# Gated linear attention: ScalarE copies the two widest levels' scores of heads 0 to 3

## The reference

```python
def gla_chunk_scan(q, k, v, log_f):
    """S_t = diag(f_t) S_{t-1} + k_t^T v_t ; o_t = q_t S_t."""
    G = jnp.cumsum(to_c(log_f), axis=3)
    ...
        o_inter = jnp.einsum('bhtk,bhkv->bhtv', qt * jnp.exp(Gt), state)
        decay = jnp.where(causal, jnp.exp(jnp.where(causal, diff, 0.0)), 0.0)
        attn = jnp.einsum('bhtk,bhsk,bhtsk->bhts', qt, kt, decay)
        o_intra = jnp.einsum('bhts,bhsv->bhtv', attn, vt)
```

## Time and profile before

| | |
|---|---|
| time, median of 3 runs | 1917.98 us (1917.0 to 1919.4) |
| the profiled execution's own time | 1920.67 us |
| its span in the trace | 1919.0 us |
| TensorE busy (matmul) | 1874.8 us, 98% |
| VectorE busy | 1177.9 us, 61% |
| ScalarE busy | 1041.1 us, 54% |
| GpSimd busy | 375.9 us, 20% |

### The profile page before, as it was taken

The page is one execution under the profiler, slowest core; times in us unless marked ns, Lnnn a source line. Parts: engine busy times, 40 slices in busy tenths (PEclk is TensorE's granted clock), DMA queues, the critical chain, the costliest instruction groups (busy, mean ns, idle before and its releaser), DMA issues.

```text
span 1919.0 us, 27344 instructions
## 1 busy us (share of the span) xinstructions
PE 1874.8 (98%) x10047; PEld 1629.7 (85%) x10047; DVE 1177.9 (61%) x2462; ACT 1041.1 (54%) x1810; POOL 375.9 (20%) x453
## 2 busy tenths in 40 slices
PE   7999999999999999999999999999999999999998
PEld 7987877788788777689999999999888887778887
DVE  3335389754799999875454554445343645957972
ACT  5654543444588887764545554555443565445440
POOL 1601233101001100132122332133020102402310
PEclk9999999999999999999999999999999999999999
DMA  4411222118699999932333233333343512122131
GB/s 155 142 56 45 67 66 67 48 63 286 215 369 360 359 372 355 333 116 61 91 84 94 80 84 93 84 90 104 98 142 112 177 55 77 56 66 77 56 110 44
DMA packets 187312, 259.44 MB, mean 135 GB/s; under 512 B 14605, under 2 KB 101594, under 8 KB 187178
## 3 DMA queue, kind: packets, MB, share of 16 engines
q1 hardware_dynamic: 178048, 225.56, 36.5%
q0 software_dynamic: 8720, 31.59, 4.4%
q10 hardware_dynamic: 410, 0.52, 0.1%
HBM read 239.24 MB, written 14.16 MB: 132 GB/s over the span
## 4 chain that ended last, share of the span: by engine, by line
PE 71%; DVE 18%; DMA 5%; ACT 3%; issue 2%; SPq 1%; POOL 0%; ACTq 0%; DVEq 0%; POOLq 0%
PE pb L2644 53%; DVE wlo L1732 7%; PE pb L2671 5%; DMA wraw<-w_down 4%; PE pb L2730 2%; PE pb L2743 2%; PE pb L3171 1%; ACT whi L1065 1%; PE pb L3279 1%; PE pb L3037 1%; SPq L796 1%; DVE arena L1993 1%; DVE AT_lo L2100 1%; PE pb L2911 1%; DVE small L1992 1%
## 5 line engine op out<-in xcount | busy, mean ns | idle before, releaser
L2644 PE MATMUL pb<-whi,AT_hi 128*128 128x512 f32 (+4 forms) x1864 | 724.8, 389 | 1.9 <-DVE arena L1928 0.8
L1732 DVE TENSOR_TENSOR wlo<-wraw,whi 128x1024 fp32r<-128x1024 f32 (+4 forms) x430 | 493.9, 1163 | 300.0 <-ACT whi L1065 297.5
L2644 PE MATMUL pb<-whi,AT_lo 128*128 128x512 f32 (+4 forms) x1864 | 677.2, 363 | 0.0
L2644 PE MATMUL pb<-wlo,AT_hi 128*128 128x512 f32 (+4 forms) x1864 | 676.1, 363 | 0.0
L1065 ACT ACTIVATE whi<-wraw 128x1024 fp32r<-128x1024 f32 (+4 forms) x446 | 440.6, 995 | 354.8 <-PE pb L2644 306.7
L2644 PEld LDWEIGHTS pb<-whi,AT_hi 128*128 128x128 f32 x1864 | 352.6, 189 | 44.3 <-issue 9.0
L2644 PEld LDWEIGHTS pb<-wlo,AT_hi 128*128 128x128 f32 x1864 | 352.9, 189 | 39.4 <-issue 6.8
L2644 PEld LDWEIGHTS pb<-whi,AT_lo 128*128 128x128 f32 x1864 | 351.6, 189 | 39.8
L2671 PE MATMUL pb<-arena 128*128 128x128 f32 (+1 forms) x956 | 144.6, 276 | 6.3 <-ACT arena L1159 2.8
L2671 PEld LDWEIGHTS pb<-arena 128*128 128x128 f32 (+1 forms) x956 | 118.2, 142 | 34.8 <-issue 7.9
L3037 PE MATMUL pb<-whi,AT_hi 128*128 128x512 f32 x256 | 104.9, 410 | 2.0 <-DVE wlo L1732 1.2
(11 more groups left out here) (363 smaller groups left out, 2624.8 us busy)
## 6 DMA issues: line engine op xcount, KB each, us to landing
wraw<-w_in_a SPq DMA_DIRECT2D x288, 128.0 KB
wraw<-w_gate SPq DMA_DIRECT2D x128, 256.0 KB
wraw<-w_up SPq DMA_DIRECT2D x128, 256.0 KB
wraw<-w_down SPq DMA_DIRECT2D x58, 512.0 KB
wraw<-w_in_b SPq DMA_DIRECT2D x40, 512.0 KB
wraw<-w_in SPq DMA_DIRECT2D x28, 512.0 KB
wraw<-w_mem_kv SPq DMA_DIRECT2D x16, 512.0 KB
wraw<-w_in_a SPq DMA_DIRECT2D x16, 512.0 KB
```

The source lines that it names most:

```text
L1732: dve.tensor_tensor(w_slot(wlo, p, p % SPL), raw_slot(p), w_slot(whi, p, p % SPL).bitcast(F32), ALU.subtract).then_inc(lo_done[p % SPL], 1)
L2644: mm = pe.matmul(ACC[bank][:, 0:n], a, b, start=kc == 0 and q == 0, stop=i == c["count"] - 1 and kk == per - 1 and q == 2)
```

## The change

In heads 0 to 3 (n below 36) VectorE's `collect` returns at once for levels 8 and 9. ScalarE makes these copies in its own stream, by the new function `wide_scores`, in steps 7 and 8 of each head: right behind `decay(n)` of the same level (in step 7 of head 0 behind the value copies too) and ahead of the next `decay`. It waits for the matmul (`gl_mm`) and for the collect of the level before (`gl_c`), and counts `gl_c` up in VectorE's place. Heads 4 to 7 are untouched.

```diff
@@ ScalarE @@
+                def wide_scores(m):
+                    lA = lAs[m // 10 % 2]
+                    act.wait_ge(S("gl_mm"), m + 1)
+                    act.wait_ge(S("gl_c"), m)
+                    if m % 10 == 8:
+                        for t in (1, 3):
+                            r = act.activation(lA[:, t - 1, P * t:P * t + P], SC[0][:, P * t:P * t + P], ACT.Copy)
+                    else:
+                        r = act.activation(lA[:, 0:2, 2 * P:4 * P], SC[1].rearrange("p (s t) -> p s t", s=2), ACT.Copy)
+                    r.then_inc(S("gl_c"), 1)
+
...
                         evac(f"vl{hh}", lambda t: lv[:, t, :], fed=True)
+                    if n < 36 and n % 9 >= 7:
+                        wide_scores(10 * (n // 9) + n % 9 + 1)
                     if n % 9 == AHEAD + 1 and n % 36 > 9:
@@ VectorE @@
                 def collect(m):
 
                     i, H = m % 10, m // 10
+                    if H < 4 and i >= 8:
+                        return
```

## The result

| | before | after |
|---|---|---|
| time, median | 1917.3 us (1915.04 to 1919.4, 10 runs) | 1926.17 us (1923.66 to 1930.9, 10 runs) |
| the profiled execution's own time and span | 1920.67, 1919.0 us | 1923.66, 1922.0 us |

The change makes the kernel slower: ratio 1.005, 95% interval 1.0042 to 1.0059, 8.9 us by the medians. The forecast was 7.0 us more, 1925.0, with a range of 1919.5 to 1929.5.

The account below looks back on a forecast made before the run. No engine was taken as full, TensorE nearest, with VectorE's copies on the path at three head ends. Ends +4.8 and clock falls +2.2 make +7.0 us on the 1917.98 median: 1925.0 us, range 1919.5 to 1929.5.

Parts of the forecast that it names:

- The new wait: At head ends, ScalarE's copies await late matmuls and hold up the next exponentials; level 9's matmul starts 2.0 us after A.
- A: At each head's end, the time at which ScalarE's copy of level 8 can start.
- The four ends: Ends of heads 0 to 3 become later by 1.2, 1.1, 0.9 and 1.6 us, sum +4.8 us.
- third step: TensorE's level 9, a tile and level 0 take 3.3 us, 4.14 before with waits; level 2 starts at A + 7.2.
- Nothing given back later: Levels 2 onward in the next head don't recover the delay, since `values_out` (20 matmuls) is next on TensorE.
- The clock: After new TensorE stops in heads 0, 1 and 3 the granted clock may fall; two of three counted, +2.2 us.
- VectorE's relief: Rival: VectorE's 1.0 us at each end of heads 0 to 2 goes, ScalarE's detour hidden; 1915.0 us, chance 0.08.
- It cancels: Rival: late head ends are caught up in the head's rest by lighter VectorE, no clock fall; 1919.9 us, chance 0.17.
- Worse handoffs: Rival: all three clock falls, GpSimd's product at 997 ns at seven handoffs, copies 0.2 us dearer; 1929.1 us, chance 0.12.

Follow-up runs that it names:

- Waits alone: Kernel before, VectorE still making all copies, with ScalarE only waiting at the two places and copying nothing: 1921.47 us beside 1917.14.
- one step later: The change with each ScalarE copy placed behind the next exponential (head 3's level 9 behind level 8's): 1914.99 us beside 1917.14 for the kernel before.
- filling the stops: The change with three throwaway 128 x 256 matmuls on TensorE between levels 8 and 9 of heads 0 to 3: 1923.39 us beside the change's 1925.33.
- level 8 only: The change with ScalarE copying level 8 only and VectorE keeping level 9: 1922.3 us beside 1917.14 for the kernel before.
- weight piece first: The change with head 0's weight piece (feed) made on ScalarE ahead of level 9's copy: 1926.38 us beside the change's 1927.54.
- VectorE held: The change with VectorE in head 2 waiting for ScalarE's copies of levels 8 and 9: 1926.29 us beside 1917.68 for the kernel before.

## Why the prediction was right

**The new wait.** Right, as worked out. Level 9's matmul was forecast at A + 2.0; in heads 1 and 3 it came at 2.01 (1653.76 to 1655.77) and 1.92 us (1690.09 to 1692.01). In heads 0 and 2 it came later, at 2.36 and 2.82 behind the copy's start, for GpSimd's longer products. Waits alone cost 4.3 us, and the same copies one step later cost nothing. (Of the 2.5 us in the earlier trace rows a weight piece, at 1683.21 in the same trace, took 1.05; the exponential still stood behind head_out's wait.) That the copies' length is no argument holds too: 599 ns on ScalarE beside 680 on VectorE, so the rule of the Trainium skill ("ScalarE: Activation LUTs", "Rules for kernel authors"), put on these copies, points to the right outcome by a reason that the runs don't bear out. I read it too widely: its row names `relu`, `max`, `min`, `add` and `mul`, and its figure for VectorE's speed is for bfloat16, so float32 copies don't contradict it.

**The four ends.** This is the term that was mis-sized. Without falls, from those executions of the change that had none there, they cost 10.07 - 7.54 = 2.5 us (forecast 1.2), 0.8 (1.1), 1.7 (0.9) and 8.32 - 6.78 = 1.5 us (1.6), together 6.6 for 4.8. (The 3.3 of the working's third step is 3.2 by its own numbers; no later figure changes by it.) Head 1's level 2 came at A + 7.2 as worked out; the end cost less because A lay 0.65 us behind level 8's start (1653.76 - 1653.11) and not 0.96. Head 0: "it has the exponents and level 0 ready early" failed, since the late weight piece also held VectorE; reordering that piece brought back 0.6 us, and GpSimd's product, 1.17 us instead of 0.8, is in the rest, of which a part stays unexplained. Head 2: the product took 1.64 us for the 0.8 assumed; holding VectorE back removed 0.7 of the 0.8 us of excess.

**Nothing given back later.** Right, to 0.02 us in the stretches between the ends.

**The clock.** Counted at 2.2 us. It is there and about that size: the medians' 8.9 less 6.6 leaves 2.3, the falls in the profiled execution make 1.7, and filling the stops gave 1.9, which the scatter doesn't confirm. That the total came near is luck in part, for its parts were wrong: a fall in head 0 costs at most 0.35 us (0.7 forecast), in head 3 1.1 to 1.4 (1.2), head 1 showed none in the three profiled executions of the change (1.4 forecast), despite a stop of about 2.05 us, and head 2, which I had excluded, had one in one of the three (1.3 us), as its stop was 1.9 us and not 1.0.

**The rivals.** VectorE's relief exists, 1.3 us by the ends and 2.5 by the medians, but needs the copies off ScalarE's path to the next exponential. "It cancels" is excluded by the stretches between the ends. "Worse handoffs" came true in part: GpSimd's product was longer in heads 0 and 2 (1.17 and 1.64 us) but not in 1 and 3 (0.82 and 0.73), the profiled execution had two falls and not three, and the copies were no dearer than assumed (275 and 599 ns). Its 1929.1 is 2.9 us above the measured time, the forecast's 1925.0 1.2 us below.

## What to carry to other kernels

Before moving work to an idle engine, look at what stands behind it in that engine's fixed order: if the moved piece waits for a late result and the piece behind it feeds an early one, the engine's lead over the pipeline is gone, whatever its load. Here an engine at 41% took 4 us of work and cost 8.9 us; one place further down it cost nothing. And cut traces at events of the program before comparing them: two executions that differ by 3 us in span hid a difference of 8.3.

## What the runs showed of the hardware

- A GpSimd product of 128 x 256 took 1.64 us beside VectorE's two-input operations in SBUF, 0.90 with fewer of them beside it, and 0.73 to 0.76 us where VectorE was idle or only made masked copies out of PSUM. In other places of the same trace the product stayed at 0.82 us and VectorE's operation took 0.94 for its 0.41. With such a product on the path, a slower VectorE made the kernel's stretch shorter.
- Whether a stop of TensorE of about 2 us is followed by a fall of the clock isn't settled by its length. The one ahead of level 1 of head 0 is 2.09 to 2.13 us in all fourteen profiled executions; a fall followed in five, before among them, and none in nine. In the six in which ScalarE's copy of level 8 makes these stops and nothing fills them (the change three times, level 8 only, weight piece first, VectorE held), a fall followed head 1's stop of 2.04 to 2.06 us in none, head 3's of 1.95 in five, and head 0's of 2.4 in four. The executions of one kernel lie between 1923.66 and 1930.9 us, the longest with the lowest mean clock.
